# Half-token layer ends, a fused bias and maximum, and an earlier eviction in a two-block model on one core

## The chip, the cores and the metric

One core of a Trainium2 chip runs the whole program. The metric is the device time of one execution in microseconds (us); smaller is better. The engines are TensorE (PE), VectorE (DVE), ScalarE (ACT), GpSimd (POOL) and SyncE (SP), which here only issues loads and stores.

## The reference, cut to what matters

The input is 512 tokens of 1024 channels in fp32. `first_block` is one layer: a Mamba-2 branch and a dilated attention branch, mixed by gates, then a gated feed-forward part, and a final RMS norm. `second_block` has two layers, each an attention and a `conv_ffn`, and each of these four ends in an RMS norm whose result is added to the stream:

```python
def rms_norm(x, gain, eps=RMS_EPS):
    y = xf * lax.rsqrt(jnp.mean(xf * xf, axis=-1, keepdims=True) + eps)
    return (y * gain.astype(jnp.float32)).astype(x.dtype)

# diff_attention, per block of 128 queries
logits = einsum(q, k) + bias ; logits = where(dist >= 0, logits, NEG_INF)
p = softmax(logits)
attn = p[:, 0] - lam * p[:, 1]          # then attn @ v, and an RMS norm per head
# forgetting_attention
decay = c[:, :, q0:k_end, None] - c[:, :, None, :k_end]
logits = einsum(q, k) + decay ; p = softmax(logits) ; p @ v

# second_block, both layers
h = h + rms_norm(a, norm_post)           # a: attention output projection
f = conv_ffn(rms_norm(h, ffn_norm_pre), ...)
h = h + rms_norm(f, ffn_norm_post)
```

`conv_ffn` multiplies by a matrix with 2 x 2816 columns, applies a causal depthwise convolution of width 3, a gelu gate, and multiplies back to 1024 columns.

## The kernel before

**Layout.** The stream is kept transposed in SBUF as `XT`: 8 chunks (`DC`) of 128 channels by 512 tokens. Every large product is made from fp32 operands split in two fp32r parts, high and low, as three products: high x high, low x high, high x low (`chunk`, L626 where the output has channels on partitions, L620 where it has tokens there). Weights come in slabs of 256 rows by 256 columns (`SLAB` = 2 chunks, `PANEL` = 256 columns). SP loads them in the order of `STREAM` into 8 `raw` buffers; POOL splits each into `whi` (L584) and `wlo` (L586), 4 buffers deep; PE frees a slab with `slab_done`. A panel of 256 output columns fills two banks of the PSUM tensor `PS`; two panels alternate, so panel p+2 waits until DVE has evicted panel p (`evicted`). The tensor `AUX` has the other four banks.

**A layer end (k = 2, 4, 6, 8, 10).** These are the norms behind `down1`, `awo`, `("fout", 0)`, `bwo` and `("fout", 1)`. `last_panel` makes the last panel's two column tiles one after the other over its last four slabs (L699). DVE copies each output tile to `branch` (L1896), ACT squares it, DVE adds the squares into `acc` (`add_squares`). Then `branch_norm` on PE: `sum_squares` sums over channels with a product against ones (L715, L720), ACT takes the root (`norm`, L1081), DVE the reciprocal (L1455), and `spread` lays the factors of all 512 tokens out over 128 partitions (L733). `keep_warm` issues bf16 products without use, 2 before and 12 after `spread` (L727). `chunks` on DVE then goes over the eight chunks: `scale` multiplies by the factor (L1912), `add` adds to `XT` (L1916; at k=2 one operation, L1889). ACT's `prepare` makes the high part of the next operand (`high`, L1077) and the squares of the next norm (L1307), and DVE the low part (`next_low`, L1435). PE's `twin_mm` uses each chunk as it comes, for the first two panels of the next product at once (for k=6 these are `k3` and the narrow `f`); the outputs are scaled later, when the next norm is known (`factors_between`, `sum_next_squares`).

**The convolution stages (`fin`).** A pair of panels belongs together: gate (half 0) and value (half 1). DVE evicts a half into `fu` (`evict`, L1931), ACT starts its convolution (L1324), DVE adds two taps per tile (`taps`, L1941), ACT applies the gelu, DVE multiplies (`products`, L1948) and makes the low part (L1952). The code of an engine is its order: DVE runs `taps(i, 0)`, `evict(i, 1)`, `taps(i, 1)`, `evict(i+1, 0)`, `products(i)`.

**The attentions (`softmax_units`, `attention`).** 32 units each: 8 tiles of two maps by 4 query blocks `qb`, with 128(qb+1) keys. `order2` writes the order: S scores on PE (L947), M bias and maximum on DVE (L2018 in the first, L2012 in the second attention, then L2021 and L2023) and the exponential on ACT (L1352), D the reciprocals and, in the first attention, the difference of the two maps (L2035 to L2039), T transposes on PE (L986) and their copies (L1362, L2027), V the product with v (L1001, L996), W the copy of its result (L2053, L2049), X the transposes of a whole tile. Slabs of the next projections are woven between as filler; in the last two tiles little filler is left. In the second attention the bias is c[t] - c[s]: `ccol` holds c per query, `negc` c per key.

## Time and profile before

| | |
|---|---|
| median of 3 runs | 2627.45 us (2625.58 to 2627.86) |
| the profiled execution | 2628.43 us, its span 2626.6 us |
| mean granted TensorE clock | 0.983 |
| PE busy | 2510.1 us |
| DVE busy | 1382.6 us |
| ACT busy | 751.3 us |
| POOL busy | 1611.8 us |
| bytes loaded from HBM | 225.29 MB, 88 GB/s over the span |

The span runs from the first to the last instruction; the execution's own time is 1.8 us longer. Durations below come from this one profiled execution. A matmul's end is modelled, so the distance between starts is its cost, not its printed duration. PEclk is the clock that TensorE was granted as a share of 2.4 GHz.

### The profile page before, as it was taken

The numbers are of one execution on the slowest core, as the hardware profiler recorded it, in microseconds if no ns is written. First come the engines' busy times: TensorE is split into PE (matmuls) and PEld (weight loads), VectorE is DVE, ScalarE is ACT, GpSimd is POOL, SyncE is SP. The second block draws the span as 40 slices with busy tenths as digits, with TensorE's granted clock in tenths as the row PEclk, the third lists the DMA queues.
The fourth block names the chain that finished last, engine by engine and source line by source line (L and its number), as shares of the span: only waits on it lengthen the run. The fifth ranks groups of instructions, "written<-read, shape, count | busy, mean of one in ns | idle before, by whom it ended". The sixth has DMA issues, their size and how long they took to land. (4 is left out here: it accounts for less than half of the span.)

```text
span 2626.6 us, 37098 instructions
## 1 busy us (share of the span) xinstructions
PE 2510.1 (96%) x12745; PEld 2071.8 (79%) x12758; DVE 1382.6 (53%) x1980; ACT 751.3 (29%) x1400; POOL 1611.8 (61%) x1548
## 2 busy tenths in 40 slices
PE   9989999999999999999999799999999989999998
PEld 7778888888877888888777587888877777778886
DVE  8567666443425433311567658773164454787712
ACT  3445453001232121100434434331032222443300
POOL 8646555754545777776544268887663333778874
PEclk9999999999999999999999899999999999999999
DMA  5323323432223333332322122333232211333321
GB/s 162 98 80 113 93 83 111 116 81 71 66 65 104 96 93 96 98 98 92 105 65 64 33 84 85 97 97 96 78 91 71 69 61 49 89 88 96 96 96 64
DMA packets 235791, 229.22 MB, mean 87 GB/s; under 512 B 15808, under 2 KB 228288, under 8 KB 235672
## 3 DMA queue, kind: packets, MB, share of 16 engines
q1 hardware_dynamic: 212224, 204.72, 26.2%
q10 hardware_dynamic: 23448, 22.84, 3.1%
q8 instruction: 83, 1.36, 0.2%
q14 instruction: 36, 0.29, 0.0%
HBM read 225.29 MB, written 4.84 MB: 88 GB/s over the span
## 5 line engine op out<-in xcount | busy, mean ns | idle before, releaser
L584 POOL TENSOR_SCALAR whi<-raw 128x512 fp32r<-128x512 f32 x772 | 558.4, 723 | 924.2 <-issue 507.0
L586 POOL TENSOR_TENSOR wlo<-raw,whi 128x512 fp32r<-128x512 f32 x772 | 1055.0, 1367 | 64.5
L626 PE MATMUL PS<-opA_hi,whi 128*128 128x512 f32 x1872 | 750.0, 401 | 16.7 <-DVE fu L1931 9.5
L626 PE MATMUL PS<-opA_hi,wlo 128*128 128x512 f32 x1872 | 734.8, 393 | 0.0
L626 PE MATMUL PS<-opA_lo,whi 128*128 128x512 f32 x1872 | 734.5, 392 | 0.0
L626 PEld LDWEIGHTS PS<-opA_hi,whi 128*128 128x128 f32 x1872 | 355.3, 190 | 105.1 <-issue 21.9
L626 PEld LDWEIGHTS PS<-opA_hi,wlo 128*128 128x128 f32 x1872 | 354.4, 189 | 75.6
L626 PEld LDWEIGHTS PS<-opA_lo,whi 128*128 128x128 f32 x1872 | 355.3, 190 | 71.3 <-issue 1.5
L1941 DVE SCALAR_TENSOR_TENSOR facc<-fu,vec,facc 128x512 f32<-128x512 f32 x176 | 208.1, 1241 | 23.4 <-ACT facc L1324 23.1
L620 PE MATMUL PS<-whi,opA_hi 128*128 128x256 f32 x704 | 207.4, 295 | 0.0
L620 PE MATMUL PS<-whi,opA_lo 128*128 128x256 f32 x704 | 200.7, 285 | 0.0
L620 PE MATMUL PS<-wlo,opA_hi 128*128 128x256 f32 x704 | 200.6, 285 | 0.0
L626 PE MATMUL PS<-hid_lo,whi 128*128 128x512 f32 x480 | 186.9, 389 | 0.0
L626 PE MATMUL PS<-hid_hi,wlo 128*128 128x512 f32 x480 | 186.9, 389 | 0.0
L626 PE MATMUL PS<-hid_hi,whi 128*128 128x512 f32 x480 | 186.9, 389 | 0.0
L620 PEld LDWEIGHTS PS<-whi,opA_hi 128*128 128x128 f32 x704 | 136.5, 194 | 7.3 <-issue 4.5
L620 PEld LDWEIGHTS PS<-whi,opA_lo 128*128 128x128 f32 x704 | 136.6, 194 | 1.4 <-issue 1.2
L1896 DVE COPY branch<-PS 128x512 f32<-128x512 f32 x32 | 21.0, 687 | 220.9 <-PE PS L626 158.8
L620 PEld LDWEIGHTS PS<-wlo,opA_hi 128*128 128x128 f32 x704 | 136.4, 194 | 0.0
L1352 ACT ACTIVATE sc<-sc,bstat 128x128 f32<-128x128 f32 (+3 forms) x128 | 70.8, 554 | 174.2 <-DVE bstat L2023 174.2
L626 PEld LDWEIGHTS PS<-hid_hi,whi 128*128 128x128 f32 x480 | 90.1, 188 | 18.7
L626 PEld LDWEIGHTS PS<-hid_hi,wlo 128*128 128x128 f32 x480 | 90.1, 188 | 18.7
(314 smaller groups left out, 3386.2 us busy)
## 6 DMA issues: line engine op xcount, KB each, us to landing
raw<-in_w_in_dram SPq DMA_DIRECT2D x184, 256.0 KB, 2.7
raw<-in_ffn_w_in_dram SPq DMA_DIRECT2D x176, 256.0 KB, 2.7
raw<-in_ffn_w_out_dram SPq DMA_DIRECT2D x88, 256.0 KB, 2.6
raw<-in_a_w_qkv_dram SPq DMA_DIRECT2D x48, 256.0 KB, 2.7
raw<-in_w_ffn_gate_dram SPq DMA_DIRECT2D x44, 256.0 KB, 2.7
raw<-in_w_ffn_up_dram SPq DMA_DIRECT2D x44, 256.0 KB, 2.7
raw<-in_w_ffn_down_dram SPq DMA_DIRECT2D x44, 256.0 KB, 2.6
acs_row<-acs_dram ACTq DMA_DIRECT2D x16, 512.0 KB, 5.7
```

What stands on the lines that cost most here:

```text
L584: nc.gpsimd.tensor_scalar(whi[slot][:], raw[raw_slot][:], 1.0, 1.0, ALU.mult, ALU.mult).then_inc(w_high, 1)
L586: nc.gpsimd.tensor_tensor(wlo[slot][:], raw[raw_slot][:], whi[slot][:].bitcast(F32), ALU.subtract).then_inc(slab_split, 1)
L620: last = nc.tensor.matmul(psum_tm(key, panel)[:, t, :], a, b[:, c, :], start=t % 2 == 0 and k + n == 0, stop=k == total - 1 and n == 2, sk ...
L626: last = nc.tensor.matmul(psum_fm(key, panel, m), a, b[:, k, :], start=k + n == 0, stop=k == total - 1 and n == 2)
L1352: A(sc[:, u % 2, e, 0:width], sc[:, u % 2, e, 0:width], ACT.Exp, bias=bstat[:, u % 4, 2 + e:3 + e], accum_out=bstat[:, u % 4, 4 + e:5 + e] ...
L1896: V.tensor_copy(branch[:, c, :], psum_fm(key, c // 2, c % 2)).then_inc(evicted, 1)
L1941: V.scalar_tensor_tensor(facc[:, j, :], fu[:, j, tap:tap + S], col("ffn_conv_w_2", 132 * l + 44 * tap + FT * half + m + 2 * i), facc[:, j, ...
```

## The change

1. **Layer ends.** `last_panel` and `branch_norm` give way to `last_panel_norm`. The second column tile of the last panel is made in two token halves (`TOKENS`), the second of them in an `AUX` bank (`tail`). For `down1` and `fout` the split in halves holds for all of the tile's slabs. Between the products of the second half PE puts the sums and the spread for the first 256 tokens. There are no warming products at the ends any more. `chunks` first treats the first 256 tokens of chunks 0 to 3 (`HALVES`), then the last 256 of the same chunks, then chunks 4 to 7 whole. `twin_mm` follows that order; between its half chunks it issues `sum_late`, `spread_late` and `spread_rest` for the other 256 tokens.
2. **ACT.** A square root of a constant (`root`) is put ahead of the root in the chain, so that the table is loaded earlier; the two exponentials for `lams` move ahead of the mix. In `prepare`, `norm_late` stands between the first high part and its squares.
3. **Attention.** `tensor_tensor_reduce` adds the bias and takes the row maximum in one instruction for each map, in place of an add and a `tensor_reduce`. In the second attention c[t] is no longer added (it is constant along a softmax row), and `ccol` with its products (L1030) falls away. In the first attention the difference of the maps is made with one pass, and the factor 1/sum of the first map is applied in W.
4. **`fin`.** `evict(i, 1)` moves from between `taps(i, 0)` and `taps(i, 1)` to behind `products(i-1)`.

The diff, cut to its core:

```diff
+HALVES = {2: 4, 4: 4, 6: 4, 8: 4, 10: 4}
...
+        first = 0
+        if norm in NEXT:
+            first = HALVES[norm - 1]
+            for h in range(2):
+                for c in range(first):
+                    for t in (a, b):
+                        s = slab_no(*t, c // SLAB)
+                        if h == 0:
+                            if c % SLAB == 0:
+                                pe.wait_ge(slab_split, s + 1)
+                            if t == a:
+                                pe.wait_ge(half_op, HALF0[norm - 1] + c + 1)
+                        elif t == a:
+                            pe.wait_ge(ready, base + c + 1)
+                        last = chunk(*t, s, c % SLAB, c, total, TOKENS[h], True)
+                        if h == 1 and c % SLAB == SLAB - 1:
+                            last.then_inc(slab_done, 1)
+                    if h == 0 and c == 0:
+                        sum_late(norm - 1)
+                    if h == 0 and c == 1:
+                        spread_late(norm - 1)
+                    if h == 0 and c == first - 1:
+                        spread_rest(norm - 1)
+        order = [(t, c) for c in range(first, total - 2) for t in (a, b)] + [(a, total - 2), (a, total - 1), (b, total - 2), (b, total - 1)]
...
+    def sum_late(k):
+        pe.wait_ge(sq_ready, SQUARES0[k] + DC + 1)
+        for t in range(2, NB):
+            last = nc.tensor.matmul(AUX[:, 1, t - 2:t - 1], sq[:, 1, t * P:(t + 1) * P], ones[:, 0:1], start=False, stop=True,
                                     skip_group_check=True)
-        if k in BRANCHES:
-            pe.wait_ge(sq_ready, SQUARES0[k] + DC)
-            for t in range(NB):
-                last = nc.tensor.matmul(AUX[:, 3, t:t + 1], sq[:, 1, t * P:(t + 1) * P], ones[:, 0:1], start=False, stop=True,
-                                        skip_group_check=True)
         last.then_inc(ss_done, 1)
+    def spread_late(k):
+        pe.wait_ge(rstd_ready, k + 1)
+        for t in range(2, NB):
+            last = nc.tensor.matmul(AUX[:, 1, t * P:(t + 1) * P], rstd_col[:, t:t + 1].broadcast_to([P, P]), ident[:], start=True, stop=True)
+        last.then_inc(bc_late, 1)
+    def spread_rest(k):
+        pe.wait_ge(half_res, HALF0[k] + HALVES[k])
+        for t in range(2, NB):
+            last = nc.tensor.matmul(AUX[:, 3, t * P:(t + 1) * P], rstd_col[:, t:t + 1].broadcast_to([P, P]), ident[:], start=True, stop=True)
+        last.then_inc(bc_done, 1)
...
+        for kk in range(first):
+            s = slab_no(key, panel, kk)
+            pe.wait_ge(slab_split, s + 1)
+            for c in range(SLAB):
+                products(psum_fm(key, panel, 0), s, c, 0, SLAB * kk + c, slice(0, S))
+                for h in range(2):
+                    last = products(tail(key, h), s, c, 1, SLAB * kk + c, TOKENS[h])
+            last.then_inc(slab_done, 1)
+        for kk in range(first, nk):
+            s = slab_no(key, panel, kk)
+            pe.wait_ge(slab_split, s + 1)
+            for c in range(SLAB):
+                last = products(psum_fm(key, panel, 0), s, c, 0, SLAB * kk + c, slice(0, S))
+        last.then_inc(first_half_done, 1)
+        for kk in range(first, nk):
+            for c in range(SLAB):
+                last = products(tail(key, 0), slab_no(key, panel, kk), c, 1, SLAB * kk + c, TOKENS[0])
+        last.then_inc(tail_done, 1)
+        pe.wait_ge(acc_ready, ADDED0[k] + DC - 1)
+        for t in range(NB):
+            nc.tensor.matmul(AUX[:, 3 if t < 2 else 1, t % 2:t % 2 + 1], acc[:, t * P:(t + 1) * P], ones[:, 0:1], start=t % 2 == 0, stop=False,
+                             skip_group_check=True)
+        for kk in range(first, nk):
+            for c in range(SLAB):
+                last = products(tail(key, 1), slab_no(key, panel, kk), c, 1, SLAB * kk + c, TOKENS[1])
+            last.then_inc(slab_done, 1)
+            if kk == first:
+                pe.wait_ge(sq_ready, SQUARES0[k] + DC)
+                for t in range(2):
+                    last = nc.tensor.matmul(AUX[:, 3, t:t + 1], sq[:, 1, t * P:(t + 1) * P], ones[:, 0:1], start=False, stop=True,
+                                            skip_group_check=True)
+                last.then_inc(ss_half, 1)
+            if kk == first + 1:
+                pe.wait_ge(rstd_half, BRANCHES.index(k) + 1)
+                for t in range(2):
+                    last = nc.tensor.matmul(AUX[:, 3, t * P:(t + 1) * P], rstd_col[:, t:t + 1].broadcast_to([P, P]), ident[:],
+                                            start=True, stop=True)
+                last.then_inc(bc_half, 1)
...
+        for c in range(HALVES[k - 1]):
+            act.wait_ge(half_res, HALF0[k - 1] + c + 1)
+            A(dst[:, c, TOKENS[0]], XT[:, c, TOKENS[0]], ACT.Copy, scale=col(name, first + c)).then_inc(half_hi, 1)
+            if c == 0:
+                norm_late(k - 1)
+            A(next_squares[:, TOKENS[0], c], XT[:, c, TOKENS[0]], ACT.Square).then_inc(next_sq, 1)
         for c in range(DC):
+            tokens = TOKENS[1] if c < HALVES[k - 1] else slice(0, S)
             act.wait_ge(res_ready, src_ready + c + 1)
-            high(dst[:, c, :], XT[:, c, :], col(name, first + c))
-            A(next_squares[:, :, c], XT[:, c, :], ACT.Square).then_inc(next_sq, 1)
+            high(dst[:, c, tokens], XT[:, c, tokens], col(name, first + c))
+            A(next_squares[:, tokens, c], XT[:, c, tokens], ACT.Square).then_inc(next_sq, 1)
...
+        A(root[:, k // 2 - 1:k // 2], ones[:, 0:1], ACT.Sqrt)
+        act.wait_ge(acc_ready, ADDED0[k] + DC - 2)
+        act.wait_ge(tail_done, BRANCHES.index(k) + 1)
+        A(sq[:, 1, TOKENS[0]], tail(key, 0), ACT.Square).then_inc(sq_ready, 1)
+        norm_half(k)
         act.wait_ge(slab_done, slab_end(key, 3))
-        squares(PS[:, 2 * ((PAN[key] + 3) % 2) + 1, :], k, DC - 1)
-        norm(k)
+        A(sq[:, 1, TOKENS[1]], tail(key, 1), ACT.Square).then_inc(sq_ready, 1)
...
+        factors_half(k)
+        for c in range(H):
+            scale(c, 0)
+            if nxt and c:
+                low_half(c - 1)
+            add(c, 0)
+            if c == (0 if k == 2 else 1):
+                late()
+            if c == 2:
+                factors_late(k)
         if nxt:
-            next_low(*nxt, DC - 1, ready0)
+            low_half(H - 1)
+        dve.wait_ge(bc_late, BRANCHES.index(k) + 1)
+        for c in range(DC):
+            tokens = TOKENS[1] if c < H else slice(0, S)
+            if c == H:
+                dve.wait_ge(bc_done, k + 1)
+            scale(c, 1 if c < H else None)
+            if nxt and c:
+                next_low(*nxt, c - 1, ready0, TOKENS[1] if c - 1 < H else slice(0, S))
+            add(c, 1 if c < H else None)
...
         evict(1, 0)
         taps(0, 1)
         products(0)
+        evict(1, 1)
         with dve.Fori(1, FP - 1) as i:
             taps(i, 0)
-            evict(i, 1)
             taps(i, 1)
             dve.wait_ge(fconv_tap, 88 * l + 8 * i + 4)
             evict(i, 0, 1)
             products(i)
+            evict(i, 1, 1)
         taps(FP - 1, 0)
-        evict(FP - 1, 1)
         taps(FP - 1, 1)
         products(FP - 1)
...
-                    dve.wait_ge(ccol_ready, 1)
-                    for e in range(2):
-                        ins = V.scalar_tensor_tensor(x[:, e], negc[:, tile % 2, e, 0:width], ccol[:, qb, 2 * tile + e:2 * tile + e + 1],
-                                                     AUX[:, e, 0:width], ALU.subtract, ALU.add)
-                    ins.then_inc(sc_ready, 1)
+                    bias = [negc[:, tile % 2, e, 0:width] for e in range(2)]
                 else:
+                    bias = [tbias[:, tile, S - width:S]] * 2
                     if u == 0:
                         dve.wait_ge(tbias_in, 16)
-                    V.tensor_tensor(x, AUX[:, 0:2, 0:width], tbias[:, tile, S - width:S].unsqueeze(1).broadcast_to([P, 2, width]),
-                                    ALU.add).then_inc(sc_ready, 1)
+                for e in range(2):
+                    ins = V.tensor_tensor_reduce(x[:, e], AUX[:, e, 0:width], bias[e], 1.0, 4.0 * NEG, ALU.add, ALU.max, st[:, e:e + 1])
+                ins.then_inc(sc_ready, 1)
                 dve.wait_ge(sc_ready, U + 1)
-                V.tensor_reduce(st[:, 0:2], x, AX.X, ALU.max).then_inc(max2, 1)
-                dve.wait_ge(max2, U + 1)
                 V.tensor_scalar(st[:, 2:4], st[:, 0:2], -1.0, None, ALU.mult).then_inc(negmax2, 1)
...
+                    V.tensor_scalar(st[:, 10:11], st[:, 7:8], lams[:, 4:5], st[:, 4:5], ALU.mult, ALU.mult).then_inc(r2_step, 1)
+                    dve.wait_ge(r2_step, r0 + 2)
                     wait(dve, tr2_done, u - 1)
-                    r0 = 4 * u
-                    dve.wait_ge(r2_step, r0 + 1)
-                    V.tensor_scalar(st[:, 10:11], st[:, 7:8], lams[:, 4:5], None, ALU.mult).then_inc(r2_step, 1)
-                    dve.wait_ge(r2_step, r0 + 2)
-                    V.tensor_scalar(dif[:, u % 2, 0:width], sc[:, u % 2, 1, 0:width], st[:, 10:11], None, ALU.mult).then_inc(r2_step, 1)
-                    dve.wait_ge(r2_step, r0 + 3)
-                    V.scalar_tensor_tensor(dif[:, u % 2, 0:width], sc[:, u % 2, 0, 0:width], st[:, 6:7], dif[:, u % 2, 0:width],
-                                           ALU.mult, ALU.subtract).then_inc(r2_step, 1)
+                    V.scalar_tensor_tensor(dif[:, u % 2, 0:width], sc[:, u % 2, 1, 0:width], st[:, 10:11], sc[:, u % 2, 0, 0:width],
+                                           ALU.mult, ALU.add).then_inc(r2_step, 1)
```

## Rows read from the trace of the kernel before

**Rows 1.** Page, busy time of the engines: us, share of the span, instructions

```profile
PE 2510.1 (96%) x12745; PEld 2071.8 (79%) x12758; DVE 1382.6 (53%) x1980; ACT 751.3 (29%) x1400; POOL 1611.8 (61%) x1548
```

**Rows 2.** Chain that ended last, in order of time: start, us, what

```profile
2222.78 10.89 PE PS L699 x48
2234.30 1.28 ACT L1081
...
2256.94 1.54 DVE opA_lo L1435
2258.52 9.81 PE PS L626 x42
```

**Rows 3.** Timeline of PE at k=8: start, us, instruction, [idle before, releaser]

```profile
2233.49 0.95 PE L715 MATMUL AUX<-ones,acc 128*128 128x1 f32 x8
...
2236.04 1.16 PE L733 MATMUL AUX<-ident,rstd_col 128*128 128x128 f32 x8 [0.19 <-DVE rstd_col L1455]
...
2240.47 0.47 PE L626 MATMUL PS<-opA_hi,whi 128*128 128x512 f32 x1 [0.69 <-DVE opA_lo L1435]
```

**Rows 4.** Timeline of DVE at the same end

```profile
2237.23 0.70 DVE L1912 TENSOR_TENSOR AUX<-branch,AUX 128x512 f32<-128x512 f32 x1 [1.25 <-PE AUX L733]
...
2239.57 0.75 DVE L1435 SCALAR_TENSOR_TENSOR opA_lo<-XT,vec,opA_hi 128x512 fp32r<-128x512 f32 x1 [0.26 <-ACT opA_hi L1077]
...
2241.85 0.75 DVE L1435 SCALAR_TENSOR_TENSOR opA_lo<-XT,vec,opA_hi 128x512 fp32r<-128x512 f32 x1 [0.26 <-ACT opA_hi L1077]
...
2251.50 1.51 DVE L1435 SCALAR_TENSOR_TENSOR opA_lo<-XT,vec,opA_hi 128x512 fp32r<-128x512 f32 x1 [0.26 <-ACT opA_hi L1077]
```

**Rows 5.** Timeline of ACT: exponentials of the first attention, then the same end

```profile
1299.68 0.51 ACT L1352 ACTIVATE sc<-sc,bstat 128x256 f32<-128x256 f32 x1 [2.71 <-DVE bstat L2023]
...
1463.40 0.19 ACT L1352 ACTIVATION_READ_ACCUMULATOR sc<-sc,bstat 128x1 f32 x1
...
2238.75 0.72 ACT L1077 ACTIVATE opA_hi<-XT,vec 128x512 fp32r<-128x512 f32 x1 [2.98 <-DVE XT L1916]
```

**Rows 6.** Chain that ended last, a slab of 24 products of 256 columns

```profile
2008.82 2.93 PE PS L620 x24
```

**Rows 7.** Timeline of POOL: the longer half of one slab's split

```profile
2236.72 1.27 POOL L586 TENSOR_TENSOR wlo<-raw,whi 128x512 fp32r<-128x512 f32 x1
```

**Rows 8.** Timelines of PE and DVE at the start of the `fin` stages

```profile
1608.40 5.18 DVE L1941 SCALAR_TENSOR_TENSOR facc<-fu,vec,facc 128x512 f32<-128x512 f32 x4 [0.26 <-ACT facc L1324]
...
1615.40 4.48 DVE L1941 SCALAR_TENSOR_TENSOR facc<-fu,vec,facc 128x512 f32<-128x512 f32 x4 [0.61 <-ACT facc L1324]
...
2292.57 2.79 DVE L1952 TENSOR_TENSOR hid_lo<-facc,hid_hi 128x512 fp32r<-128x512 f32 x2
...
2302.09 0.79 PE L626 MATMUL PS<-opA_hi,whi 128*128 128x512 f32 x1 [4.73 <-DVE fu L1931]
```

**Rows 9.** Groups of DVE by form: count, busy us, mean ns, idle before

```profile
L2021 DVE TENSOR_REDUCE bstat<-sc 128x2 f32<-128x1024 f32 x16 | 19.5, 1220 | 0.5
L2012 DVE SCALAR_TENSOR_TENSOR sc<-negc,ccol,AUX 128x512 f32<-128x512 f32 x16 | 11.2, 744 | 4.7 <-PE AUX L950 4.7
L2018 DVE TENSOR_TENSOR sc<-AUX,tbias 128x1024 f32<-128x1024 f32 x8 | 9.7, 1217 | 0.0
L2012 DVE SCALAR_TENSOR_TENSOR sc<-negc,ccol,AUX 128x256 f32<-128x256 f32 x16 | 7.0, 477 | 0.5
```

**Rows 10.** Waits of PE: waiting line, releaser: us in total, times, longest

```profile
PE AUX L1001 <- ACT pT L1362: 9.2, 5, 2.6
PE AUX L986 <- DVE osb L2049: 8.9, 8, 2.8
```

**Rows 11.** Stretches: us, busy PE, PEld, DVE, ACT, POOL, PEclk, DMA share, GB/s

```profile
2164.00:2168.00 4.00, 4.00 (x20) 3.44 (x21) 0.63 (x2) 1.35 (x5) 0.00 (x0) 0.50 0.02 4
2303.00:2306.00 3.00, 3.00 (x8) 2.33 (x8) 3.00 (x6) 0.06 (x1) 0.00 (x0) 0.50 0.00 0
```

**Rows 12.** Timeline of PE: the first record of L1030 (14 in all)

```profile
1957.65 0.40 PE L1030 MATMUL AUX<-fz,tri 128*128 128x16 f32 x2 [2.45 <-DVE fr L2091]
```

More of the change, by code:

```diff
@@ new lines, in last_panel_norm, with products @@
+            def last_panel_norm(key, k):
+                panel, nk = 3, len(SPLIT[key])
+                hi, lo = operand(key)
+                first = nk - LAST_FOUR
+                total = SLAB * nk
+                def products(dst, s, c, m, n0, tokens):
+                    ah, al = whi[s % SPL][:, c, m * P:(m + 1) * P], wlo[s % SPL][:, c, m * P:(m + 1) * P]
+                    for n, (a, b) in enumerate(((ah, hi), (ah, lo), (al, hi))):
+                        last = nc.tensor.matmul(dst, a, b[:, n0, tokens], start=n0 + n == 0, stop=n0 == total - 1 and n == 2)
+                    return last
+                wait(pe, evicted, 2 * (PAN[key] + panel) - 2)
+                for kk in range(first):
[36 more added lines that the diff above has]
+                        last.then_inc(bc_half, 1)
@@ L1271, in _ @@
                     A(o1_hi[:, h, qb * P:(qb + 1) * P], AUX[:, 3, 0:P], ACT.Copy).then_inc(o1_high, 1)
+            act.wait_ge(lam_step, 3)
+            for n in range(2):
+                A(lams[:, 2 + n:3 + n], lams[:, n:n + 1], ACT.Exp).then_inc(lam_act, 1)
             act.wait_ge(o1_ready, 16)
@@ L1864, in _, with next_low @@
             add_squares(2, 6)
-            done("down1", 3)
-            down_residual(7)
-            def next_low(name, first, c, ready0):
+            dve.wait_ge(tail_done, 1)
+            V.tensor_tensor(XT[:, DC - 1, TOKENS[0]], XT[:, DC - 1, TOKENS[0]], tail("down1", 0), ALU.add).then_inc(evicted, 1)
+            def next_low(name, first, c, ready0, tokens):
                 dve.wait_ge(res_ready, ready0 + c + 1)
-                low(opA_lo[:, c, :], XT[:, c, :], col(name, first + c), opA_hi[:, c, :])
@@ L1873, in chunks @@
-            def chunks(scale, add, k, ready0, nxt, first):
-                factors_done(k)
-                scale(0)
-                add(0)
-                for c in range(1, DC):
-                    scale(c)
-                    if nxt:
-                        next_low(*nxt, c - 1, ready0)
-                    add(c)
-                if nxt:
-                    next_low(*nxt, DC - 1, ready0)
+                low(opA_lo[:, c, tokens], XT[:, c, tokens], col(name, first + c), opA_hi[:, c, tokens])
```

169 lines of the change are left out of this document (112 added, 57 removed).

## The prediction

> **What bounds the kernel now.** I read the page first: TensorE (PE) is busy for 96% of the span [rows 1], so the change can only pay where PE waits or runs slowly. Then the chain that ended last. It is PE nearly everywhere, but at each layer end it leaves PE for about 24 us and goes through ACT and VectorE (DVE) until the twin products run on by themselves [rows 2]. The timelines of PE, DVE and ACT around one layer end give the steps [rows 3 to 5]. The other places are two stalls at the start of the `fin` stages and the last tiles of both attentions [rows 8 to 11].
>
> Take the end after `bwo` (k=8). The last panel ends with 48 products in 10.89 us, 0.227 each [rows 2]; the last 24 are the second column tile. PE starts the sums at 2233.49 [rows 3], so this tile began at T0 = 2233.49-24x0.227 = 2228.05. Times with a plus sign are counted from there. Before: PE is through at +5.44, DVE's first scaling is at +9.18, and the first product of the next layer at +12.42, a gap of 6.98 us that sums, spreads and warming products partly fill [rows 3, 4]. But PE does not wait again, and the eighth `opA_lo` starts at 2256.94 and lets the last 18 twin products go at 2258.52, so the twin ends at 2258.52+18x0.227 = 2262.6, or +34.55. DVE's chain of eight chunks, not PE's gap, sets this end: per chunk the add (0.75), ACT's `opA_hi` (0.72), and the low part (0.75, the next instruction 0.67 after its start) give 2.27 us, the distance of the first two L1435 rows [rows 4, 5].
>
> **The layer ends, worked out.** Prices: a 256-column product costs 2.93/24 = 0.122 us against 0.227 for 512, so each pair costs 0.017 more [rows 2, 6]. A DVE operation on 256 columns takes 0.48 (the L2012 form [rows 9]), and the next starts 0.40 after it; ACT on 256 columns takes 0.51 [rows 5]. The handovers (DVE to ACT 0.04, ACT to DVE 0.10, DVE to PE 0.15) are distances between the rows of [rows 3 to 5].
>
> New order, after T0: 24 half products to +2.9; eight sum records 0.85 to +3.8; six half products, the sum of the first half's square (0.5) to +5.0; root, reciprocal (no table load is left there) to +5.65; PE fits in six products until +5.8 and then the spread (0.5). So the first scaling stands at +6.45, 2.7 us earlier. ACT, however, may prepare the next operand only after the second half's square, which waits for the end of all products at +7.7; its first `opA_hi` is at +8.3 and the first low half at +8.9 to +9.3. PE starts the twin at +9.5: its gap is 1.75 us instead of 6.98.
>
> Then comes what I think decides it. After that first half chunk ACT waits in `norm_late` for `sum_late`, which PE issues only behind the 12 half products of chunk 0: 9.5+1.46+0.5, root 0.2, the square of the half (about 0.6), second `opA_hi` 0.5: the second low half starts at +12.9, PE resumes at +13.5 after 2.1 us idle. Behind this wait stand all further `opA_hi`, hence DVE's lows. From there a half chunk costs 0.48+0.04+0.51+0.10+0.40 = 1.53 us, which is more than half of 2.27. Lows of the first half end at +16.4; the second halves of chunks 0 to 3 have their lows at +17.95 and every 1.53 to +22.5; full chunks follow at +24.55 and every 2.27; the eighth low ends at +32.1. In the same count, without collisions with POOL, before ends at +28.2; its real +30.4 is 2.2 later, since lows that meet POOL's split take up to 1.51 us for 0.75 [rows 4]. If the same comes again in part (1.5), the eighth low is done at +33.6 and the twin at +37.8. PE's own sum (9.5, 96 half and 48 full products, three sums and spreads, the idle 2.1 and 0.7) gives +36.3. I take the middle of the two, +37.6: **3.1 us later** than before for k=4 and 8. For k=6 the twin is narrow (`f` has one column tile), DVE alone sets the end, +3.8; for k=2 ACT also waits for the late add, +3.6. Together 13.6. Bounds: with no collision and PE's ordering perfect, an end could gain 2.7 (all idle time gone); with collisions as before and a full extra wait of a wlo pass at the first low, it loses 5.
>
> At k=10 nothing follows: four half chunks at 0.86, four more, four full ones at 1.39 from +6.45 end at +19.6, against 2624.2 or +20.4 before: -0.8. The split tile also costs 42 pairs x 0.017 = 0.7 in each of the three long panels (`down1`, two `fout`): +2.2. The removed table load is counted in the root above; where ACT idles (`lams` exponentials before the mix) it costs nothing. Layer ends in all: **+15.0**.
>
> POOL is moved too: slabs of the last panel now come free at +4.5, +5.8, +7.0 and +7.7 instead of from +1.4 on. The longer half of a split takes 1.27 [rows 7], and I take 1.95 for the whole of it, so the twin's first four slabs are ready by +12.5, before PE wants the fourth at about +15; in the second pass the fifth slab is freed for at +21.1 and wanted at +24.8. No wait, but POOL is busy while the first lows run, which it was not before.
>
> Here a rule speaks against the change. The rows show a low of 1.51 against 0.75 [rows 4]. The Trainium skill, SBUF — State Buffer, section Who interferes with whom, says that a VectorE operation with two SBUF inputs and a GpSimd operation that reads SBUF exclude each other for the whole instruction. The trace agrees with that. By it twelve lows in place of eight meet POOL more often, and an end would come out up to about 1 us worse than my 1.5 for collisions.
>
> **The `fin` stages.** Before, PE waits 4.73 us for the eviction of panel 3's successor, L1931, because DVE does four taps first, and then 12 products run with the clock at 0.50 (1.2 GHz) after that idle stretch, 8 starts in 3 us, 0.43 instead of 0.23 each [rows 8, 11]: 4.73+2.45 = 7.2. With the eviction behind `products(0)` (second pair begins 2292.57, ends 2295.36) it is done at 2296.7, before PE needs it at 2302.09-4.73 = 2297.4. What is late next is `evict(2, 0)`: taps(1,0) and taps(1,1) take 11.5 us (1608.40 to 1619.9 [rows 8]), so it ends at 2296.7+11.5+1.3 = 2309.5 and with the loop's entry a little later, where PE wants it 48 products after 2297.4, at 2308.2; about 1.8 us stay, too short, I take it, to bring the clock down. Later iterations have slack, and in the last one the taps that now follow PE's last panel are hidden: `fout` reads that chunk at the end of a panel of 132 products, 30 us later. Gain 5.4 each, two stages: **-10.8** (bounds -7 and -14.4).
>
> **Attention.** One `tensor_tensor_reduce` per map replaces add and maximum. No row shows it. Nearest: an add of 512 columns at 0.69 to 0.74, two of them 1.41, and 1.22 for the reduction of both that falls away [rows 9]. So a unit of full width goes from 2.44 to 1.41 in the first attention and from 2.63 to 1.41 in the second, and D loses one pass of 0.5 (up to 1.0 where it meets POOL). Lower end of its price: the add's time, 0.7. Upper end: 1.2, so that two cost what both old ones did. I take the add's time plus 0.1 to 0.2, since ACT shows a separate record of 0.19 after each accumulating exponential [rows 5]. The Trainium skill, VectorE: DVE Perf Modes, section on two Vector instructions with no wait between them, says the same of VectorE, an accumulator output is two instructions; whether this one shows a second record no run here shows yet. That DVE saves time matters only where PE waits for it. In the bulk PE waits 0.7 us at a time, mostly for handovers that stay: -0.5, and -0.3 at the first units. In the last two tiles it matters: waits up to 2.6 for `pT` behind exponentials behind the maximum, up to 2.8 for `osb` behind it [rows 10], with stretches at clock 0.50 after them [rows 11]. First attention: three of those waits shrink by 1.8, 2.0 and 1.0, less 1 for accumulators, and half of the 4.8 us that the low clock costs returns: -6.5. Second: 0.95, 1.2, 0.9, less 1, and two thirds of 3.3: -4.3. The cumulative columns no longer made (L1030, 14 records, half of a 5.4 us stretch [rows 12]) give 2.7, of which the low clock that outlasts them takes back 0.7: -2.0. In all **-13.6** (bounds -3 and -21).
>
> **Sum.** +15.0 - 10.8 - 13.6 = -9.4. The profiled execution took 2628.4 us (span 2626.6), so 2619.0; the median of the runs, 2627.45, is 1.0 lower: 2618.0.
>
> **Rivals.** (a) The ends gain what they promise: 2.7 each at four ends with ACT's wait hidden. For it: PE's pure work does end there. Against: the chain ran through DVE, not PE [rows 2]. -10.8+1.4-24.4: 2594. (b) The fused operation is as slow as the two it replaces, 1.2 us for 512 columns. Nothing in the trace excludes it; all two-input rows at 0.7 speak against. Then the attention gives only L1030 and D's pass, about -3.5: +0.7, 2628. (The Trainium skill, Vector Engine (DVE) Microarchitecture Reference, Points that are easy to get wrong, states half rate for an accumulating two-tensor operation with two non-bf16 SBUF sources; here one source is PSUM, so by its wording it would not apply.) (c) Slower: PE's two gaps of 1.75 and 2.1 us with 1.5 us of work between them bring the clock to 1.2 GHz, as waits of 2.5 and 2.8 us did in the attention and as the warming products, now gone, prevented. Then chunk 0 takes 1.5 us longer inside ACT's wait and the following 5.4 us of products double: about +6 at each of four ends, 24 in all: 2642. It decides from 2.4 us per end, where the forecast's gain is used up. (d) The reordered eviction only shifts the stall with its low clock to `evict(2, 0)`: +7 to +8, 2625.
>
> **Chances.** Forecast 0.58, (a) 0.12, (b) 0.13, (c) 0.08, (d) 0.09. 0.2% is 5.3 us, about what a measurement of this kernel can tell from no change. Within the forecast (-9.4, give or take 6) some four in five are beyond that: faster 0.58x0.8+0.12+0.03 = 0.62; same 0.58x0.18+0.13x0.7+0.05 = 0.24; slower 0.14. The range leaves out the far half of (a) and (c): 2602 to 2633.
>
> **What would show it.** Right: PE's first gap at an end 1.5 to 2 us, a second of about 2 us behind the first 12 half products, released by ACT or the low half; twin ends 2 to 5 us later after T0; no 4.7 us wait at L1931's successor but one near 2 us; DVE's fused rows 0.7 to 0.9 for 512 columns; clock 1.00 in both tails. Wrong: no second gap, a low clock at the ends, or fused rows near 1.2.

## Result and profile after the change

The changed kernel takes 2633.91 us (median of 19 runs), the kernel before in the same comparison 2627.86: the ratio is 1.0023, with an interval of 1.0016 to 1.0030. It is slower by 6 us, where I had forecast 2618, 10 us faster. The profiled execution has a span of 2631.4 us. Its busy line on the page, to be read against [rows 1]:

```profile
PE 2512.7 (95%) x13112; PEld 2089.1 (79%) x13120; DVE 1317.3 (50%) x2106; ACT 757.9 (29%) x1445; POOL 1611.8 (61%) x1548
```

DVE has lost 65 us of work and PE has gained 2.6, so the attention did become cheaper for DVE, and the total still rose. **The layer end at k=8**, in the timeline of PE after the change (start, us, instruction, idle before and releaser):

```profile
2231.90 0.28 PE L787 MATMUL PS<-opA_hi,whi 128*128 128x256 f32 x1
...
2234.78 0.95 PE L811 MATMUL AUX<-ones,acc 128*128 128x1 f32 x8
...
2241.07 0.36 PE L639 MATMUL PS<-opA_hi,whi 128*128 128x256 f32 x1 [1.51 <-DVE opA_lo L2005]
...
2245.05 0.58 PE L639 MATMUL PS<-opA_hi,whi 128*128 128x256 f32 x1 [1.97 <-DVE opA_lo L2005]
...
2274.14 0.95 PE L752 MATMUL AUX<-ones,acc 128*128 128x1 f32 x8
```

T0 is 2231.90 here. The one gap of [rows 3] has become two, of 1.51 and 1.97 us. The same end in the timelines of DVE and ACT, DVE first:

```profile
2238.18 0.43 DVE L2083 TENSOR_TENSOR AUX<-branch,AUX 128x256 f32<-128x256 f32 x1 [0.89 <-PE AUX L826]
...
2244.13 0.87 DVE L2005 SCALAR_TENSOR_TENSOR opA_lo<-XT,vec,opA_hi 128x256 fp32r<-128x256 f32 x1 [2.14 <-ACT opA_hi L1417]
...
2263.58 0.75 DVE L1554 SCALAR_TENSOR_TENSOR opA_lo<-XT,vec,opA_hi 128x512 fp32r<-128x512 f32 x1 [0.86 <-ACT opA_hi L1172]
```

ACT:

```profile
2243.12 0.17 ACT L1184 ACTIVATE std<-AUX 128x2 f32<-128x2 f32 x1 [2.73 <-PE AUX L759]
...
2243.63 0.47 ACT L1417 ACTIVATE opA_hi<-XT,vec 128x256 fp32r<-128x256 f32 x1
```

The first scaling is at +6.28 instead of +9.18 [rows 4], but ACT idles 2.73 us for `sum_late` (L759), and the last low part ends at +32.4, against +30.4 before. **Fused bias and maximum**, groups of DVE by form (count, busy us, mean ns, idle before): an instruction and a short second record, in place of the first two rows of [rows 9]:

```profile
L2197 DVE DVE_READ_ACCUMULATOR2_ANT bstat<- 128x1 f32 x128 | 10.5, 82 | 0.0
L2197 DVE CUSTOM_DVE_ANT_0 sc<-AUX,negc 128x512 f32<-128x512 f32 x16 | 10.4, 687 | 4.7 <-PE AUX L1048 4.7
```

**The `fin` start and the tail of the first attention**, timeline of PE, against [rows 8] (4.73) and [rows 10]:

```profile
1469.75 0.78 PE L1045 MATMUL AUX<-k,q 64*128 64x128 f32 x4 [3.06 <-DVE bstat L2197]
...
1496.53 1.14 PE L1099 MATMUL AUX<-v,pT 128*128 128x128 f32 x6 [3.83 <-ACT pT L1484]
...
2316.34 0.76 PE L639 MATMUL PS<-opA_hi,whi 128*128 128x512 f32 x1 [2.13 <-DVE fu L2113]
```

**Where the time went.** I cut each span at T0 of the five ends and at the sum of the next norm (PE reading `ones,acc`; at k=8 that is 2274.14 above, and this row of before):

```profile
2268.17 0.95 PE L715 MATMUL AUX<-ones,acc 128*128 128x1 f32 x8
```

| stretch, us | before | after | after less before |
|---|---|---|---|
| start to the sum of k=1 | 908.6 | 913.6 | +5.0 |
| `ffn1`, `down1` to T0 of k=2 | 336.4 | 339.7 | +3.3 |
| end k=2 | 40.5 | 43.1 | +2.6 |
| first attention, `awo` | 240.4 | 235.0 | -5.4 |
| end k=4 | 39.9 | 42.3 | +2.4 |
| `fin`, `fout` 0 | 335.3 | 335.5 | +0.2 |
| end k=6 | 37.8 | 42.5 | +4.7 |
| second attention, `bwo` | 289.2 | 280.3 | -8.9 |
| end k=8 | 40.1 | 42.2 | +2.1 |
| `fin`, `fout` 1 | 335.7 | 335.5 | -0.2 |
| end k=10 | 22.8 | 21.8 | -1.0 |

The first two stretches hold no part of the change but the two early exponentials and 0.7 us of split tile, and lose 8.3. The cause shows when PE alone is asked how many instructions it had in 50 us of full clock. Stretches of PE (us, busy, count, PEclk, DMA share, GB/s), the first in `fin`, which reads `opA`, the second in `fout`, which reads `hid`; before:

```profile
1650.00:1700.00 50.00, 50.00 (x223) 1.00 0.33 95
1815.00:1865.00 50.00, 50.00 (x223) 1.00 0.31 99
```

and after:

```profile
1650.00:1700.00 50.00, 50.00 (x222) 1.00 0.33 94
1815.00:1865.00 50.00, 50.00 (x216) 1.00 0.28 93
```

Products of one shape on one engine at one clock start at 0.2267 us before, and at 0.2333 after where they read `hid`. (Here and below a pitch is the mean distance of starts within all unbroken rows of products of a tensor, 1263 or more for `hid`; a count in a window has up to two extra from the modelled ends.) The same holds for `yT`, `o` and `mix`; `opA` stays at 0.2269. The change contains one line that displaces them all:

```diff
         subg = r.put("subg", [P, 1])
+        root = r.put("root", [P, 8])
         dsk = r.put("dsk", [P, NH])
```

`root` takes 32 bytes of each partition; everything allocated behind it, up to `XT`, moves up by 32, while `whi`, `wlo` and `opA` lie ahead of it. (Only `negc`, which DVE reads, also moves down by the 256 bytes of `ccol`.) The first stretch has 672 displaced products and the second 462. At 0.0066 each that is 4.4 of its 5.0 us and 3.0 of its 3.3. `XT` itself has a fixed address.

### The profile page after: what moved, and what is told of

The parts are those of the page before. It is cut to its first block and busy times, and to the rows that moved or that the text cites. A ratio compares the mean times of both kernels' runs of the same rounds, so it can differ in the third digit from the quotient of the medians.

```text
span 2631.4 us, 37972 instructions
## 1 busy us (share of the span) xinstructions
PE 2512.7 (95%) x13112; PEld 2089.1 (79%) x13120; DVE 1317.3 (50%) x2106; ACT 757.9 (29%) x1445; POOL 1611.8 (61%) x1548
## 5 line engine op out<-in xcount | busy, mean ns | idle before, releaser
L639 PE MATMUL PS<-opA_hi,whi 128*128 128x512 f32 (+1 forms) x1932 | 761.5, 394 | 27.7 <-DVE opA_lo L2005 14.5
L639 PE MATMUL PS<-opA_lo,whi 128*128 128x512 f32 (+1 forms) x1932 | 745.0, 386 | 0.0
L639 PE MATMUL PS<-opA_hi,wlo 128*128 128x512 f32 (+1 forms) x1932 | 745.0, 386 | 0.0
L639 PEld LDWEIGHTS PS<-opA_hi,wlo 128*128 128x128 f32 x1932 | 367.2, 190 | 72.9
L639 PEld LDWEIGHTS PS<-opA_lo,whi 128*128 128x128 f32 x1932 | 367.9, 190 | 68.9 <-issue 1.5
L639 PE MATMUL PS<-hid_hi,whi 128*128 128x512 f32 x396 | 156.4, 395 | 0.0
L639 PE MATMUL PS<-hid_hi,wlo 128*128 128x512 f32 x396 | 156.4, 395 | 0.0
L639 PE MATMUL PS<-hid_lo,whi 128*128 128x512 f32 x396 | 156.4, 395 | 0.0
L1964 DVE TENSOR_TENSOR facc<-PS,rstd_bc 128x512 f32<-128x512 f32 x42 | 27.1, 686 | 138.2 <-PE PS L639 138.0
L639 PEld LDWEIGHTS PS<-hid_hi,wlo 128*128 128x128 f32 x396 | 74.2, 187 | 18.3
```

The costliest lines, as they stand in the source:

```text
L639: last = nc.tensor.matmul(psum_fm(key, panel, m)[:, tokens], a, b[:, k, tokens], start=tokens.start == 0 and k + n == 0, stop=k == total - ...
L1964: V.tensor_tensor(facc[:, 2 * half + m, :], psum_fm("ffn1", half, m), rstd_bc[:], ALU.mult).then_inc(evicted, 1)
```

## Experiments

Medians against the kernel before in the same series, whose median was 2627.27 (e1 to e4), 2628.05 (e5 to e8), 2628.00 (e9 to e11) and 2627.84 (e12 to e15).

| run | median | less before | ratio, interval |
|---|---|---|---|
| e1 | 2622.16 | -5.1 | 0.9981, 0.9972 to 0.9990 |
| e2 | 2648.55 | +21.3 | 1.0078, 1.0064 to 1.0092 |
| e3 | 2607.79 | -19.5 | 0.9924, 0.9910 to 0.9937 |
| e4 | 2618.60 | -8.7 | 0.9964, 0.9952 to 0.9977 |
| e5 | 2620.21 | -7.8 | 0.9971, 0.9961 to 0.9982 |
| e6 | 2662.46 | +34.4 | 1.0132, 1.0117 to 1.0148 |
| e7 | 2672.74 | +44.7 | 1.0172, 1.0156 to 1.0187 |
| e8 | 2598.73 | -29.3 | 0.9894, 0.9878 to 0.9909 |
| e9 | 2628.18 | +0.2 | 1.0002, 0.9993 to 1.0012 |
| e10 | 2634.11 | +6.1 | 1.0026, 1.0016 to 1.0035 |
| e11 | 2647.76 | +19.8 | one run |
| e12 | 2621.83 | -6.0 | 0.9979, 0.9970 to 0.9988 |
| e13 | 2648.40 | +20.6 | one run |
| e14 | 2631.65 | +3.8 | one run |
| e15 | 2606.82 | -21.0 | 0.9924, 0.9910 to 0.9937 |

### The displaced tensors: e1 and e2

```diff
# e1, on the changed kernel
-        root = r.put("root", [P, 8])
+        root = r.put("root", [P, 16])
# e2, on the kernel before
+        gap = r.put("gap", [P, 8])
         dsk = r.put("dsk", [P, NH])
```

> The changed kernel with one edit: the new small tensor `root` is 64 bytes per partition instead of 32, so that every tensor behind it (yT, o, mix, hid, opB, XT's neighbours) starts again at a multiple of 64 bytes as in the kernel before. Theory A: the distance between 512-column products that read these tensors, 0.233 us after the change against 0.227 before, comes from the start at 32 bytes past a multiple of 64. Then 2250 such products each lose 0.0067 us: 15.0 us less than the changed kernel, 2633.9 - 15.0 = 2618.9. Rival B: the distance comes from something else in the new instruction stream (more instructions, another order): no change, 2634.

> The kernel before with one edit: an unused tensor of 32 bytes per partition in the place where the change puts `root`. Theory A: 2448 products go from 0.227 to 0.233 us, +16.3: 2644. Rival B: 2628, unchanged.

Thirty-two unused bytes cost the kernel before 21.3 us, and 32 more took 11.8 from the changed one. Rival B is out. Of the 21.3, the slower products explain 2448 x 0.0066 = 16.2. The same stretches taken of e2 put another 1.1 into end k=2 and 2.4 into the first attention. In both the granted clock was lower than before: 0.57 in e2 from 1262 to 1266 and from 1306.5 to 1310.5, and 1.00 at the same two places of the kernel before (1251 to 1255, 1295.6 to 1299.6). Why it fell there is not shown. In e1 the pitch did not go all the way back; it was 0.2290 with `hid` (PE's stretch in `fout`, e1):

```profile
1815.00:1865.00 50.00, 50.00 (x220) 1.00 0.30 95
```

### Which address counts: e6, e7, e9

```diff
# e6
+        gap0 = r.put("gap0", [P, 8])
         opA_hi = r.put("opA_hi", [P, DC, S], F32R)
         opA_lo = r.put("opA_lo", [P, DC, S], F32R)
+        gap1 = r.put("gap1", [P, 8])
# e7: gap0 ahead of whi, gap1 between wlo and opA_hi
# e9: gap0 ahead of whi alone
```

> The kernel before with 32 unused bytes ahead of opA_hi and opA_lo, and 32 behind them, so that only these two and no other tensor start at 32 past a multiple of 64. Theory A1: any moving operand of 512 columns that starts so costs 0.0067 us more. 5712 products read opA as moving operand: +38, 2665. Rival A2: it is a matter of the region in which yT, o, mix, hid and opB lie (where they stand against the weights), not of the start as such: +0 to +5. DVE's low parts and ACT's high parts also write to these addresses, which neither bounds here.

> The kernel before with 32 unused bytes ahead of the split weights whi and wlo and 32 behind them. They are the loaded operand (stationary) of all 512-column products and the moving operand of 2112 products of 256 columns. Theory A1, only moving operands pay and the price is one fixed amount for each product: 2112 x 0.0067 = +14, 2642, and no change in the distance of the 512-column products. If loading pays too, 8160 products go slower and the time is above 2680. If 256 columns do not pay, 2628.

> The kernel before with 32 unused bytes ahead of whi and wlo and none behind them: weights, opA and all tensors behind them move by 32 bytes together. Theory A3, formed after e6 and e7 (both made the products between weights and opA slower, 0.2333 against 0.2269, though one moved only the moving operand and the other only the loaded one): what counts is the distance between the loaded and the moving operand modulo 128 bytes, not where either starts. Then nothing changes: 2628, pitch 0.227. Theory A1, the start of either operand at 32 past a multiple of 64 costs: all 8160 products at 0.2333 or more, above 2670.

PE's stretches, e6:

```profile
1650.00:1700.00 50.00, 50.00 (x216) 1.00 0.33 94
1815.00:1865.00 50.00, 50.00 (x220) 1.00 0.32 95
```

e7:

```profile
1650.00:1700.00 50.00, 50.00 (x216) 1.00 0.33 94
1815.00:1865.00 50.00, 50.00 (x216) 1.00 0.32 95
```

e9:

```profile
1650.00:1700.00 50.00, 50.00 (x222) 1.00 0.32 94
1815.00:1865.00 50.00, 50.00 (x222) 1.00 0.32 96
```

In e6 `opA` is slow (0.2333), in e7, where all tensors behind the weights stand 32 bytes further from them, every 512-column product is; in e9 all have moved by 32 and nothing is slow. A1 falls: it would have made all of e9's products slow. What counts is the distance between the operand that is loaded and the one that streams. (In e6 the two gaps put `hid` 64 bytes further on, and it stands at 0.2289, as in e1.) My expectation for e7 (2642, for the 256-column products alone) had these wrong as well: with the weights moved they went from 0.1197 to 0.1183 us, a little faster. The Trainium skill, TensorE: Matmul & The Clock Gate, section Step-by-step: what each phase is for, says that loading the next tile's weights takes no SBUF read bandwidth from the running product, since the two have ports of their own. By that no distance between the two could matter, and e6 and e7 would have come out at 2628 like e9. They are 34.4 and 44.7 us slower, and the measurement decides.

### Which distances are good: e10, e11, e13, e14, and e12

```diff
# e10: root of [P, 32], 128 bytes, on the changed kernel
# e11, e13, e14: gap of [P, 24], [P, 48], [P, 64] on the kernel before, in e2's place
# e12, on the changed kernel: root in unused space, no tensor displaced
+        root = r.put("root", [P, 8])
         r.at = norm_tmp + 8 * KB
```

> The changed kernel with `root` taking 128 bytes per partition instead of 32. In e1 it took 64, and the products that read hid, mix, o and yT still stood at 0.2290 where the kernel before has 0.2267. With 128 every distance modulo 128 is that of the kernel before. Theory A3: 2250 products lose another 0.0023 us: 5.2 less than e1, 2617. Rival: 64 was enough and the rest is something else: 2622.

> The kernel before with 96 unused bytes in the place of `root`: distance 96 modulo 128 between the weights and yT, o, mix, hid, opB. One look at the pitch. If the price goes by the distance modulo 64: 0.2333 as with 32. If by the distance modulo 128: a value of its own, between 0.2267 and 0.24.

> The kernel before with 192 unused bytes in the place of `root`. One look at the pitch of the products that read hid. So far: 0 bytes 0.2267, 32 0.2333, 64 0.2290, 96 0.2334, 128 0.2333 (e10). If 64 is better because it is a certain distance from a multiple of 256, 192 is either like 64 (0.229) or like 128 (0.233).

> The kernel before with 256 unused bytes in the place of `root`. If the distance between loaded and moving operand counts modulo 256 bytes, the pitch is 0.2267 again and the time 2628. If it does not return, only the distances that are multiples of a larger power of two are good, or the first address was good by chance: 0.229 to 0.2333, 2633 to 2648.

> The changed kernel, all four parts, with `root` in unused space ahead of rstd_bc, so that every tensor of the kernel before has exactly the address that it had there. The theory that my error of 16 us is the displaced tensors alone: 2250 products at 0.2267 instead of 0.2333, 14.8 less than the changed kernel, 2619, which is my forecast of 2618 within its noise. If 32 bytes were only part of it, 2622 or more.

| displacement, bytes | 0 | 32 | 64 | 96 | 128 | 192 | 256 |
|---|---|---|---|---|---|---|---|
| pitch with `hid`, us | 0.2267 | 0.2333 | 0.2290 | 0.2334 | 0.2333 | 0.2333 | 0.2267 |

The same stretch of PE in e10:

```profile
1815.00:1865.00 50.00, 50.00 (x216) 1.00 0.30 93
```

and in e14:

```profile
1815.00:1865.00 50.00, 50.00 (x223) 1.00 0.32 99
```

My modulus of 128 (in theory A3 of e9's expectation) was wrong: 128 bytes are as bad as 32 for `hid`, and at 256 the pitch is that of 0. The code of the kernel before gives these displacements a meaning. Added up from the first weight buffer, the addresses of `opA`, `yT`, `o`, `mix`, `hid` and `opB` all lie at whole multiples of 256 bytes from every weight buffer. So each displacement in the table is the distance itself modulo 256, and the fast case is a whole multiple. Why 64 costs a third of what the others do, and 192 the whole, no run tells. e14's only run took 3.8 us more than the kernel before all the same. Its first attention is 3.0 longer, and the granted clock was 0.51 there from 1296.5 to 1300, where before it was 1.00. e12 gives the answer that the case turns on: with every old tensor but `negc` at its old address the full change is **6.0 us faster** than the kernel before, interval 0.9970 to 0.9988, and 12.1 better than the change as made. Of the 2250 x 0.0066 = 14.9 expected, 2.8 are missing. In e12's profiled execution the clock was low in end k=2, where it was full after the change; that end took 44.9 us there against 43.1. The second attention took 283.2 against 280.3: the clock was at half for two spells near its start (0.50 from 1960.5 to 1963.9 and from 1970.7 to 1974.1), after the change for one. Stretches of all engines (us, busy PE, PEld, DVE, ACT, POOL, then PEclk, DMA share, GB/s), e12, from 8.2 us after T0 of k=2:

```profile
1252.00:1262.00 10.00, 6.87 (x33) 6.81 (x34) 3.30 (x8) 4.45 (x10) 4.29 (x5) 0.60 0.35 99
```

and after, the same place, then a piece of end k=8:

```profile
1261.50:1271.50 10.00, 6.89 (x57) 6.84 (x58) 4.60 (x11) 5.66 (x13) 4.28 (x5) 1.00 0.31 98
2244.00:2248.00 4.00, 2.95 (x14) 2.95 (x15) 3.02 (x7) 2.82 (x6) 0.72 (x1) 0.58 0.48 134
```

### The parts of the change: e3 and e5

e3 is the kernel before with the attention and `fin` hunks of the diff alone, e5 with the `fin` hunk alone.

> The kernel before with only parts 3 (attention) and 4 (eviction order in fin) of the change; the layer ends stay as they were and the tensors keep their places. By the trace after, the stretches of both attentions are 5.4 and 9.0 us shorter than before, the second although 1.3 us of slower products lie in it, and the fin stretches about 3 us each after the slower products are taken off: 5.4 + 10.3 + 6.2 = 21.9 less than before, 2606. If the gains of the attention hung on the new layer ends, less than half of it would come, above 2617.

> The kernel before with part 4 alone (the eviction order in fin). Of the 19.5 us that parts 3 and 4 brought together, the fin stretches of e3 are 4.7 and 3.5 us shorter than before (from the sum after the layer end to the last panel's second column tile). So 8 less than before, about 2619; by my prediction 10.8 less, 2617. If the two parts only pay together, less than 4.

The `fin` order brings 7.8, so the attention is left with 11.6 (of 19.5, before rounding), and the layer ends cost 19.5 - 6.0 = 13.5 (e12 against e3). The attention part and the layer ends have no run of their own; both are differences of runs. The profiled executions divide the gains otherwise. In e5 the two stretches of `fin` and `fout` are 4.7 and 5.0 us shorter than before, 9.7 in all, and the second attention, which the edit does not touch, is 2.1 longer. Part of that is a spell at half clock (0.50 from 1965.4 to 1968.4; 1.00 at the same place before, 1970.8 to 1973.8). In e3 the first attention is 3.8 shorter and the second 10.1. The stall of 2.13 us at the second eviction stands in both stages of e3, e5, e12 and the changed kernel. The clock behind it was at half in both stages of the changed kernel and of e12, in one of e3 and in none of e5. The stretch right behind the stall, after the change and in e5:

```profile
2316.50:2319.50 3.00, 3.00 (x8) 2.32 (x9) 2.75 (x5) 2.04 (x3) 0.22 (x1) 0.50 0.39 106
2307.30:2310.30 3.00, 2.99 (x13) 2.48 (x14) 2.74 (x4) 1.87 (x3) 0.39 (x1) 1.00 0.41 128
```

### What holds the layer ends: e4 and e15

```diff
# e4 on e1; e15 on e12 together with e8
                     first = HALVES[norm - 1]
+                    sum_late(norm - 1)
                     for h in range(2):
...
-                            if h == 0 and c == 0:
-                                sum_late(norm - 1)
```

> As e1, and PE makes the sum for tokens 256 to 511 (`sum_late`) ahead of the first half chunk instead of behind it, in the gap in which it waits for the first low half anyway. My theory of the second gap: ACT waits there for this sum, behind PE's 12 half products. Then the gap of 2.0 us closes, the second low half comes 2 us earlier and with it DVE's whole chain: -2.0 at each of four ends, 8 us less than e1, about 2611. Rival: the chain is then held by collisions with GpSimd's splits, which move into the same stretch: -0.5 an end, 2 less than e1.

> e12 with `sum_late` ahead of the first half chunk (e4) and the gate half evicted ahead of the value taps (e8): all parts of the change at their best, against e8, which has the old layer ends. If the new ends with the early sum cost nothing, 2599 or less. By the stretches of e4 they still cost 0.8 + 1.5 + 2.7 + 1.2 at the four ends and some 2 in the split tiles, less 1 at the last: +7, 2606.

The second gap closes. In e4 ACT waits 0.36 us instead of 2.73 for the late sum, and DVE starts the second low half at 2229.71, which is +10.0 after its T0 (2219.70) instead of +12.2. ACT's timeline in e4, and DVE's behind it:

```profile
2228.55 0.17 ACT L1183 ACTIVATE std<-AUX 128x2 f32<-128x2 f32 x1 [0.36 <-PE AUX L758]
```

```profile
2229.71 1.16 DVE L2004 SCALAR_TENSOR_TENSOR opA_lo<-XT,vec,opA_hi 128x256 fp32r<-128x256 f32 x1
2231.84 1.16 DVE L2004 SCALAR_TENSOR_TENSOR opA_lo<-XT,vec,opA_hi 128x256 fp32r<-128x256 f32 x1 [0.18 <-ACT opA_hi L1416]
...
2250.38 0.89 DVE L1553 SCALAR_TENSOR_TENSOR opA_lo<-XT,vec,opA_hi 128x512 fp32r<-128x512 f32 x1 [0.86 <-ACT opA_hi L1171]
```

So the wait that I named was real. But the second and third low half, which took 0.87 and 0.48 us after the change, now take 1.16. Each runs while GpSimd makes a `wlo`, and ends 0.28 us behind it. POOL's timeline in e4:

```profile
2229.30 1.29 POOL L599 TENSOR_TENSOR wlo<-raw,whi 128x512 fp32r<-128x512 f32 x1
...
2231.43 1.29 POOL L599 TENSOR_TENSOR wlo<-raw,whi 128x512 fp32r<-128x512 f32 x1
```

The last low part ends at +31.6, only 0.9 earlier. The run came out 3.6 us below e1, between the 8 of my theory and the 2 of the rival. Part of this gain is the clock. It was at half for a spell in the ends k=2, 4 and 6 of e1 (0.51, 0.50, 0.50), and it is 1.00 in all four ends of e4. At k=8 it was full in both, and the end is 1.3 us shorter. The chain that ended last tells what bounds the end at k=8. After the change it holds PE's own work alone from the end of the second gap (2245.05) to the sum; its last piece before the sum is

```profile
2257.65 16.65 PE PS L639 x72
```

In e4 it runs through DVE, as before the change, down to the last low part:

```profile
2250.38 0.90 DVE opA_lo L1553
2251.33 9.81 PE PS L639 x42
```

With the clock full, e4's four ends are still 0.7, 1.4, 2.6 and 1.2 us longer than before. Against e8, e15 shows what the new ends cost at their best: 8.3 us. They lose with the wait and without it.

### A version that beats both: e8

```diff
                     taps(i, 0)
-                    taps(i, 1)
                     dve.wait_ge(fconv_tap, 88 * l + 8 * i + 4)
                     evict(i, 0, 1)
+                    taps(i, 1)
                     products(i)
```

> As e3 (parts 3 and 4 on the kernel before), and in the loop of fin DVE evicts the gate half of the next pair ahead of the taps of the value half instead of behind them. Panel (2,0) is done about 2297.4 at k=8 and wanted at 2308.2; DVE gets to it 5.7 us earlier. Theory: the stall of 2.13 us at the second eviction goes, and the slow clock that follows it in some stages: -2.1 to -4 each in two stages, 4 to 8 less than e3, about 2602. Rival: DVE, which now waits in every pair for PE's panel before it may do the value taps, comes late with the next eviction: 0.3 us or more lost in each of 20 pairs, slower than e3.

2598.73 us, 29.3 below the kernel before. e3 stood 19.5 below it, so this order brings 9.8, more than the 4 to 8 expected. In the profiled executions 6.4 of it lie in the two `fin` and `fout` stretches and 1.5 in the ends k=6 and k=8. There e3's clock was at half for a spell (0.50) and e8's was 1.00, so that part is not the order's. In e5, timeline of PE, the stall at the second eviction still stands, as after the change:

```profile
2307.31 0.47 PE L626 MATMUL PS<-opA_hi,whi 128*128 128x512 f32 x1 [2.13 <-DVE fu L1931]
```

In e8 DVE makes that eviction at 2296.85, ahead of the value taps at 2299.21, and PE waits for `fu` in neither stage:

```profile
2291.70 5.03 DVE L1937 SCALAR_TENSOR_TENSOR facc<-fu,vec,facc 128x512 f32<-128x512 f32 x4
2296.85 1.29 DVE L1927 TENSOR_TENSOR fu<-PS,rstd_bc 128x512 f32<-128x512 f32 x2
2299.21 4.97 DVE L1937 SCALAR_TENSOR_TENSOR facc<-fu,vec,facc 128x512 f32<-128x512 f32 x4 [1.07 <-ACT facc L1321]
```

Both stretches of `fin` and `fout` take 328.2 us, against 330.6 and 332.2 in e3. The rival (DVE late in every pair) did not come.

## Why the prediction was wrong

**The step that failed** is the first price, "0.227 for 512" columns. I took it from rows of before and let it stand for the kernel after, where the displaced products cost 0.2333, since nothing about the products of `yT`, `o`, `mix`, `hid` and `opB` was changed. I priced `root` as a table load and not as 32 bytes of SBUF. That term stood at nothing in the sum, and so in the rivals and the range. It is worth 12.1 us (e12), and with it the same sum gives 2630, on the other side of the kernel before. That the sum then comes within 4 us of the measured time does not prove its other terms. Term by term, from e3, e5 and e12:

- **Layer ends**, +15.0 forecast, +13.5 measured. At k=8 the forecast steps were first scaling +6.45 (measured +6.28), first gap 1.75 (1.51), second low half +12.9 (+12.2), second gap 2.1 (1.97), eighth low done +32.1 to +33.6 (+32.4). The ends lengthened by 2.6, 2.4, 4.7 and 2.1 (forecast 3.6, 3.1, 3.8, 3.1), and k=10 gained 1.0 (0.8). The wait of ACT for `sum_late` is shown by e4. Behind it my two sums, PE's and DVE's, were nearly equal (+36.3 and +37.8), and which of them ends last differs: PE's at k=8 of the changed kernel, with two gaps and a spell at half clock in it, DVE's in e4. DVE's distance of 1.53 us for a half chunk came as forecast (the lows at 2250.16, 2251.69 and 2253.21). That GpSimd's splits lengthen the low parts fits e4's rows, where the longer ones end 0.28 behind a `wlo`; no run took the splits away. My terms for k=10 add up to +18.9 and not +19.6.
- **`fin`**, -10.8 forecast, -7.8 measured. The stall of 4.73 went and one of 2.13 came (forecast 1.8), at the eviction that I had named. I took that stall for too short to bring the clock down. It did so in both stages after the change and in e12, in one of e3's, and in none of e5's; e3's stretch without it is 330.6, the one with it 332.2, so it costs 1.6. In e5 the two stretches gained 9.7 of the 10.8; the rest of its shortfall is the 2.1 in the second attention.
- **Attention**, -13.6 forecast, -11.6 measured. The -11.6 is a difference of medians; in e3's profiled execution the two attention stretches are 13.9 shorter. The fused form costs 0.687 plus a second record of 0.082, and starts lie 0.61 apart, somewhat less than the 0.7 plus 0.1 that I took; rival (b) is out. The tails were divided wrongly. The stretch of the first gained 3.8 in e3, where I had 6.5 for its tail alone: the waits did not shrink one by one, they merged into 3.06 and 3.83, behind the new maximum and behind `pT`. (The parts of that 6.5 add up to 6.2.) The second gained 10.1, where I had about 7 with its start. The sign "clock 1.00 in both tails" did not come: after the change it was 0.50 from 1470 to 1476.5 and from 2173 to 2176.4. These spells are only shorter than before (0.50 from 1461 to 1471 and from 2164 to 2170.5).
- **Rival (c)**, the clock at the ends, had the event right and its price too high. Before, the clock was full (1.00) in the ends k=2 to k=8. After the change it was at half for a spell in three of these four (k=4, 6 and 8; 0.58 in the stretch at 2244 above), in e12 in all four. The two readings of end k=2 put it at 1.8 us, not 6.
- **Rival (a)** is out; (d) holds in part, as said under `fin`.

## What to carry to other kernels

When a change adds or resizes any buffer, compare the addresses of the tensors behind it first, and the distance of starts of an untouched kind of product in the trace: the same instruction at another pitch is an address, not a schedule. Keep a matmul's two operands at the distance modulo 256 bytes at which the kernel was tuned (here a whole multiple of 256), and put new small tensors where they displace nothing. And halving chunks to start a chain earlier pays only where the start bounds it. Here the start came 2.9 us earlier and the end later: the halves brought a second wait, and a half chunk takes 1.53 us on DVE, two thirds of a whole one (2.28).

## What the runs showed of the hardware

- The pitch of 512-column fp32r products goes by the distance in SBUF between loaded and moving operand, with a period that fits 256 bytes: 0.2267 us at whole multiples of 256, up to 0.2334 at other distances, 2.9%, and no change when both move together (e9). Only distances that differ by multiples of 32 bytes were tried, and the 64-byte value (0.2290) fits no simple rule.
- 256-column products go the other way: 0.1197 at the good distance and 0.1183 at 32 bytes off (e6, e7); those that read `hid` 0.1197 (e12) and 0.1167 (after).
- The fused add and maximum with PSUM and SBUF sources runs in 0.687 us for 512 columns, no more than the add alone [rows 9], and leaves a second record of 0.082.
- The same wait on PE can be followed by either clock. Behind the 2.13 us stall in `fin` the granted clock was 0.50 after the change and 1.00 in e5; with two waits of 1.6 to 2.1 us in end k=2 it stayed at 1.00 after the change and was 0.60 in e12. This moves single stretches by 1 to 2 us from run to run.
